# A fused two-block transformer kernel: each feed-forward's down product by seven products for a pair of chunks instead of eight

## The reference, cut to what matters

```python
# first block: x is 272 x 1024 (16 meta tokens ahead of 256), D_FF = 2816
h = rms_norm(x, ffn_norm_g[l])
g = jnp.einsum('bld,df->blf', h, w_gate[l])
u = jnp.einsum('bld,df->blf', h, w_up[l])
x = x + jnp.einsum('blf,fd->bld', jax.nn.silu(g) * u, w_down[l])
return x[:, N_META:]
# second block: D_FF_2 = 4096
n2 = rms_norm_2(h, norm_mlp_pre[l])
hid = jnp.square(jax.nn.relu(jnp.einsum('bsd,df->bsf', n2, w_up[l])))
mlp_out = jnp.einsum('bsf,fd->bsd', hid, w_down[l])
h = h + rms_norm_2(mlp_out, norm_mlp_post[l])
```

## Time and profile before

| | us |
|---|---|
| time, median of 3 runs (lowest to highest) | 759.55 (758.77 to 761.12) |
| the profiled execution's own time | 758.59 |
| its span, first to last instruction | 757.3 |
| PE busy | 739.8 (98%) |
| DVE, ACT, POOL busy | 457.8, 373.3, 112.5 |
| first feed-forward's products, start to end | 131.0 to 321.0 |
| second feed-forward's products, start to end | 570.2 to 751.5 |

### The profile page before, as it was taken

How to read it: one execution, slowest core, us unless ns; L and a number is a source line. 1 busy time by engine, 2 the same in 40 slices (tenths; PEclk the granted TensorE clock), 3 DMA queues, 4 the chain that set the end, 5 groups by cost and what they waited for, 6 DMA issues and landing times.

```text
span 757.3 us, 11043 instructions
## 1 busy us (share of the span) xinstructions
PE 739.8 (98%) x4394; PEld 641.1 (85%) x4394; DVE 457.8 (60%) x635; ACT 373.3 (49%) x535; POOL 112.5 (15%) x138
## 2 busy tenths in 40 slices
PE   6999999999999999999999999999999999999996
PEld 5877778999999999888888888888779899998895
DVE  5898695766555555465747555674948754455433
ACT  6666754644444434285443534664338644444431
POOL 2867550100000000001110000000302111001110
PEclk9999999999999999999999999999999999999999
DMA  9642142787665666446536543474535766656511
GB/s 318 207 132 82 58 160 92 229 284 220 189 212 172 195 216 208 133 142 219 169 110 195 194 139 112 123 250 147 178 107 198 260 192 187 206 184 191 180 46 56
DMA packets 70179, 130.46 MB, mean 172 GB/s; under 512 B 5312, under 2 KB 29072, under 8 KB 70128
## 3 DMA queue, kind: packets, MB, share of 16 engines
q1 hardware_dynamic: 68144, 125.00, 52.3%
q0 software_dynamic: 1552, 4.20, 1.7%
q10 hardware_dynamic: 432, 0.56, 0.2%
HBM read 128.62 MB, written 1.05 MB: 171 GB/s over the span
## 4 chain that ended last, share of the span: by engine, by line
PE 93%; DVE 3%; DMA 2%; issue 1%; ACT 1%; SPq 0%; DVEq 0%; ACTq 0%
PE psum L453 41%; PE psum L888 29%; PE psum L506 12%; PE psum L930 2%; DMA w_raw<-in_w_in 2%; PE psum L680 1%; PE psum L601 1%; PE psum L546 1%; PE psum L631 1%; PE psum L1058 1%; PE psum L582 1%; PE psum L652 1%; DVE b_ratio L2154 0%; PE psum L992 0%; PE psum L1020 0%
## 5 line engine op out<-in xcount | busy, mean ns | idle before, releaser
L1908 DVE TENSOR_TENSOR w_lo<-w_raw,w_hi 128x1024 fp32r<-128x1024 f32 x225 | 275.2, 1235 | 158.3 <-ACT w_hi L1284 157.7
L1284 ACT ACTIVATE w_hi<-w_raw 128x1024 fp32r<-128x1024 f32 x231 | 241.2, 1059 | 180.7 <-PE psum L888 78.6
L888 PE MATMUL psum<-h_hi,w_hi 128*128 128x256 f32 x608 | 170.3, 284 | 0.6 <-issue 0.6
L888 PE MATMUL psum<-h_hi,w_lo 128*128 128x256 f32 x608 | 169.5, 283 | 0.0
L888 PE MATMUL psum<-h_lo,w_hi 128*128 128x256 f32 x608 | 161.8, 281 | 0.0
L888 PEld LDWEIGHTS psum<-h_hi,w_hi 128*128 128x128 f32 x608 | 114.7, 189 | 1.7 <-issue 0.7
L888 PEld LDWEIGHTS psum<-h_hi,w_lo 128*128 128x128 f32 x608 | 114.4, 188 | 0.0
L888 PEld LDWEIGHTS psum<-h_lo,w_hi 128*128 128x128 f32 x608 | 111.1, 189 | 0.7
L453 PE MATMUL psum<-w_hi,h_hi 128*128 128x512 f32 (+1 forms) x240 | 94.5, 394 | 0.0
L453 PE MATMUL psum<-w_hi,h_lo 128*128 128x512 f32 (+1 forms) x240 | 93.0, 387 | 0.0
L453 PE MATMUL psum<-w_lo,h_hi 128*128 128x512 f32 (+1 forms) x240 | 92.9, 387 | 0.0
(11 more groups left out here) (303 smaller groups left out, 992.7 us busy)
## 6 DMA issues: line engine op xcount, KB each, us to landing
w_raw<-in_w_in SPq DMA_DIRECT2D x77, 512.0 KB, 4.5
w_raw<-in_w_down SPq DMA_DIRECT2D x54, 512.0 KB, 4.3
w_raw<-in_w_up SPq DMA_DIRECT2D x32, 512.0 KB, 4.4
w_raw<-in_w_gate SPq DMA_DIRECT2D x44, 256.0 KB, 2.9
w_raw<-in_w_up SPq DMA_DIRECT2D x44, 256.0 KB, 3.4
w_raw<-in_w_out SPq DMA_DIRECT2D x16, 512.0 KB, 4.0
w_raw<-in_w_branch_a SPq DMA_DIRECT2D x4, 512.0 KB, 4.6
w_raw<-in_w_branch_b SPq DMA_DIRECT2D x4, 512.0 KB, 4.6
```

The costliest lines, as they stand in the source:

```text
L888: mm = pe.matmul(outs, x[:, cols], y[:, kc, :], start=kc == 0 and n == 0, stop=kc == KC - 1 and n == (1 if i == 0 else 2))
L1284: act.activation(T.w_hi[:, k % SLOTS, :], T.w_raw[:, k % RAW_SLOTS, :], ACT.Copy).then_inc(S.w_rounded, 1)
L1908: dve.tensor_tensor(T.w_lo[:, k % SLOTS, :], T.w_raw[:, k % RAW_SLOTS, :], T.w_hi[:, k % SLOTS, :], ALU.subtract).then_inc(S.w_cut, 1)
```

## The change

Two chunks of the inner width (a pair), two halves of the tokens and two halves of the output make a 2 x 2 by 2 x 2 block product. Before, it takes eight products of 128 x 128 by 128 x 512; now it takes seven, in the manner of Strassen and Winograd, of sums and differences of the blocks. The last pair of each feed-forward still takes eight (`down_quarters`).

- **Weights.** `w_down` is laid out as four quarters of 128 x 512 a pair (`quarters`). POOL loads them: three as they are (`load_pair`, 768 KB), the fourth twice (`load_twice`, 512 KB written), and on these two it adds the first two by a transfer that accumulates (`add_pair`, `accum_op`, 512 KB). DVE makes two more sums (`sum_pair`, `sum_pair_rest`). So ACT rounds and DVE cuts seven matrices of 512 columns in three parts (`round_pair`, `cut_pair`: 1536, 1024 and 1024 columns), where it had been two fills of 1024. The results lie in two buffers of their own; the fills now have 4 slots in a feed-forward.
- **Hidden rows.** DVE makes four differences (`sum_hidden`, `_2`, `_3`), ACT rounds and DVE cuts seven blocks (896 columns).
- **PSUM.** Products use banks 0 to 6, and the up products, laid out in fills of one 128-column group, have bank 7 alone. ACT copies it out (`take_up`, in the second block relu by `take_hidden`; the square is now ACT's too), and PE waits for that (`up_taken`) before the next pair of groups.
- **The start of a feed-forward** (`up_first`) works through two banks first: it needs the first and second fill at once and then, after a quarter of the work, the third and the fourth.
- **The ends.** Four of the last products are closed (`MIXED`), and DVE makes the output quarters from the seven sums (`form`, `add_x`) while PE does the three others and the last pair. In the first block three quarters are done before PE turns `x`, and the fourth after.

The diff, cut to its core (without the blank lines):

```diff
+        for f in range(2 * PAIRS1):
+            self.first["up1", f] = len(self.fills)
+            for w in range(2):
+                self.fills.append([(lambda raw: raw, a["up1"][f, :, w, :])])
...
+PRODUCT = {1: (1, 0, 2), 2: (3, 2, 0), 3: (7, 1, 1), 4: (2, 6, 6), 5: (5, 3, 5), 6: (6, 5, 3), 7: (4, 4, 4)}
+EARLY, LATE, MIXED, OWN = (1, 2, 3), (7, 5, 6, 4), (1, 6, 7, 5), (4, 2, 3)
+NEEDS = {1: 1, 2: 1, 3: 1, 7: 2, 5: 2, 6: 3, 4: 3}
+QUARTERS = {1: ((0, 0, 6), (1, 0, 0), (1, 1, 1), (0, 1, 7)), 2: ((0, 0, 6), (0, 1, 7), (1, 0, 0), (1, 1, 1))}
+def pair_place(q):
+    i = q if q <= LAST1 else q - FIRST2
+    return (i + 1) % 2, i % 2
...
-        def multiply_down(i, first):
-            for c in range(chunks):
-                k = W.first[down, i] + c
-                pe.wait_ge(*W.cut(S, k))
-                if c % 2 == 0:
-                    pe.wait_ge(S.hidden_cut, cut0 + i * cut_per + c // 2 + 1)
-                mm = chunk(T.hid_hi[i % 2], T.hid_lo[i % 2], k, 0, 1, c, ((4, 5), (6, 7)), WIDE, first and c == 0, False)
-                mm.then_inc(S.w_used, 1)
...
-            if i > 1:
-                pe.wait_ge(*taken(i - 1))
...
+    def up_first(name, ready, rounded, spread, right=None):
+        k0 = W.first[name, 0]
+        for s, two in ((0, 0), (1, 0), (0, 1), (1, 1), (2, 0), (2, 1), (3, 0), (3, 1)):
+            ks = (k0 + 2 * two, k0 + 2 * two + 1)
+            if s == 0:
+                for k in ks:
+                    pe.wait_ge(*W.cut(S, k))
...
+    def down(q, products, first=False, last=False):
+        buf, i = pair_place(q)
+        pe.wait_ge(S.hidden_cut, q + 1)
+        for n_product, p in enumerate(products):
+            x, y, b = PRODUCT[p]
+            pe.wait_ge(S.pair_cut, pair_parts(q) + NEEDS[p])
+            x_hi, x_lo = T.hid_hi[:, i, x - 1, :], T.hid_lo[:, i, x - 1, :]
+            y_hi, y_lo = T.pair_hi[buf][:, y, :], T.pair_lo[buf][:, y, :]
+            for n, (u, v) in enumerate(((x_hi, y_hi), (x_hi, y_lo), (x_lo, y_hi))):
+                mm = pe.matmul(bank[b][:], u, v, start=first and n == 0, stop=last and n == 2)
+            if last:
+                mm.then_inc(S.product_done, 1)
+        if products == LATE:
+            mm.then_inc(S.pair_used, 1)
+    def down_quarters(block, some):
+        q = (LAST1, LAST2)[block - 1]
+        buf, i = pair_place(q)
+        pe.wait_ge(S.hidden_cut, q + 1)
+        pe.wait_ge(S.pair_cut, pair_parts(q) + 2)
+        for t, half, b in some:
+            if b == 7:
...
+    up_first("up1", CUT["h2"], NORM["h2"], True, turn_x_right)
+    up_two(W.first["up1", 2], 3)
+    pe.wait_ge(S.up_taken, 2)
+    up_two(W.first["up1", 3], 7)
+    up_two(W.first["up1", 4], 6)
+    for i in range(2, PAIRS1):
+        if i == 2:
+            pe.wait_ge(S.spread_copied, 1)
+        else:
+            pe.wait_ge(S.up_taken, 2 * i)
+            up_two(W.first["up1", 2 * i], 7)
+        down(i - 2, EARLY, first=i == 2)
+        pe.wait_ge(S.up_taken, 4 if i == 2 else 2 * i + 1)
+        up_two(W.first["up1", 2 * i + 1], 7)
+        if i == 2:
+            pe.wait_ge(S.up_taken, 5)
+        down(i - 2, LATE, first=i == 2)
+    down(LAST1 - 1, MIXED, last=True)
+    down(LAST1 - 1, OWN)
+    down_quarters(1, QUARTERS[1][:3])
+    turn_pairs(T.x, (0, 1), (5, 6), [[(S.x_added, 9)], [(S.x_added, 10)]])
+    down_quarters(1, QUARTERS[1][3:])
...
+    up_first("up2", CUT["h4"], NORM["h4"], False)
+    up_two(W.first["up2", 4], 3)
+    for i in range(2, PAIRS2):
+        if i > 2:
+            pe.wait_ge(S.up_taken, 2 * PAIRS1 + i)
+            up_two(W.first["up2", 2 * i], 7)
+        else:
+            pe.wait_ge(S.up_taken, 2 * PAIRS1 + 2)
+        down(FIRST2 + i - 2, EARLY, first=i == 2)
+        if i == 2:
+            pe.wait_ge(S.up_taken, 2 * PAIRS1 + 3)
+        down(FIRST2 + i - 2, LATE, first=i == 2)
+    down(LAST2 - 1, MIXED, last=True)
+    down(LAST2 - 1, OWN)
+    down_quarters(2, QUARTERS[2])
...
+    def round_pair(q, part):
+        buf, i = pair_place(q)
+        if part == 0:
+            act.wait_ge(S.pair_landed[i], pair_loads(q))
+            if q == 1:
+                act.wait_ge(S.w_used, W.first["up1", 2])
+            elif q == FIRST2:
+                act.wait_ge(S.quarter_done, 4)
+            elif q == FIRST2 + 1:
+                act.wait_ge(S.w_used, W.first["up2", 4])
+            elif q > 1:
+                act.wait_ge(S.pair_used, pairs_used(q - 1))
+        elif part == 1:
+            act.wait_ge(S.pair_added[i], pair_adds(q))
+        else:
+            act.wait_ge(S.pair_summed, pairs_summed(q) + 1)
...
+    def take_up(j):
+        act.wait_ge(S.w_used, W.first["up1", j] + 2)
+        if j > 1:
+            act.wait_ge(S.hidden_done, j - 1)
+        src = T.psum[:, 4 + 2 * j:6 + 2 * j, 0:SEQ] if j < 2 else halves({2: 3, 4: 6}.get(j, 7))
+        act.activation(T.rows[:, j % 2, :].rearrange("p (c n) -> p c n", c=2), src, ACT.Copy).then_inc(S.up_taken, 1)
...
+    for i in range(1, PAIRS1):
+        round_pair(i - 1, 0)
+        take_up(2 * i)
+        round_fill(f + 4 * i + 4)
+        silu(2 * i)
+        round_fill(f + 4 * i + 5)
+        round_hidden(i - 1)
+        round_pair(i - 1, 1)
+        round_pair(i - 1, 2)
+        if i == LAST1:
+            round_quarters(LAST1, 0)
+            round_quarters(LAST1, 1)
+        take_up(2 * i + 1)
+        round_fill(f + 4 * i + 6)
+        silu(2 * i + 1)
+        round_fill(f + 4 * i + 7)
...
+    def sum_pair(q):
+        i = pair_place(q)[1]
+        dve.wait_ge(S.pair_cut, pair_parts(q) + 1)
+        dve.wait_ge(S.pair_added[i], pair_adds(q))
+        step(dve.tensor_tensor(T.pair_raw[i][:, 0, :], T.pair_t[:, i, 0, :], T.pair_raw[i][:, 1, :], ALU.add))
+    def sum_pair_rest(q):
+        i = pair_place(q)[1]
+        own()
+        dve.tensor_tensor(T.pair_raw[i][:, 2, :], T.pair_raw[i][:, 0, :], T.pair_raw[i][:, 2, :],
+                          ALU.add).then_inc(S.pair_summed, 1)
+    def sum_hidden(q, done):
+        h = T.hbuf[:, pair_place(q)[1]]
+        dve.wait_ge(S.hidden_done, done)
+        if q > 1:
+            dve.wait_ge(S.hidden_cut, q - 1)
+        step(dve.tensor_tensor(h[:, 4:6, :], h[:, 0:1, :].broadcast_to([P, 2, P]), h[:, 1:3, :], ALU.subtract))
...
+    for i in range(1, PAIRS1):
+        sum_hidden(i - 1, 2 * i)
+        cut_pair(i - 1, 0)
+        sum_hidden_2(i - 1)
+        scale_gate(2 * i)
+        sum_hidden_3(i - 1)
+        cut_fill(f + 4 * i + 4)
+        sum_pair(i - 1)
+        times_up(2 * i)
+        sum_pair_rest(i - 1)
+        cut_fill(f + 4 * i + 5)
+        cut_hidden(i - 1)
+        cut_pair(i - 1, 1)
+        cut_pair(i - 1, 2)
+        if i == LAST1:
+            cut_quarters(LAST1, 0)
+            cut_quarters(LAST1, 1)
+        scale_gate(2 * i + 1)
+        cut_fill(f + 4 * i + 6)
+        times_up(2 * i + 1)
+        cut_fill(f + 4 * i + 7)
+    cut_hidden(LAST1)
...
+    p1, u, v21, v22, v12 = T.form[1]
+    dve.wait_ge(S.first_copied, 1)
+    form(1, 2, 3, p1, u, ALU.subtract)
+    step(add_x(p1, 1, 0))
+    own()
+    form_minus(1, 3, 4, u, v21)
+    form(1, 4, 5, u, v12)
+    own()
+    step(add_x(v21, 0, 0))
+    form(1, 4, 5, v21, v22, ALU.subtract)
+    step(add_x(v12, 1, 1))
+    own()
+    step(add_x(v22, 0, 1))
+    for n, (t, half, b) in enumerate(QUARTERS[1]):
+        dve.wait_ge(S.quarter_done, n + 1)
+        own()
+        add_x(bank[b][:], t, half).then_inc(S.x_added, 1)
...
+    round_fill(f + 4)
+    round_pair(FIRST2, 0)
+    round_fill(f + 5)
+    round_pair(FIRST2, 1)
+    round_pair(FIRST2, 2)
+    take_hidden(0)
+    take_hidden(1)
+    square_hidden(0)
+    square_hidden(1)
+    round_fill(f + 6)
...
+            round_pair(q, 0)
+            round_hidden(q)
+            round_pair(q, 1)
+            if k < len(W.fills):
+                round_fill(k)
+            round_pair(q, 2)
+            take_hidden(i)
+            square_hidden(i)
+            if k < len(W.fills):
+                round_fill(k + 1)
...
+    def end_last(n):
+        t, half, b = QUARTERS[2][n]
+        dve.wait_ge(S.quarter_done, 4 + n + 1)
+        own()
+        dve.tensor_tensor(T.last[t, half], bank[b][:], T.last[t, half], ALU.add).then_inc(S.formed, 1)
...
+    end_last(0)
+    scale_last(0)
+    end_last(1)
+    scale_last(1)
+    post_mean(1, 0)
+    end_last(2)
+    post_add(1, 0, HALVES)
+    scale_last(2)
+    end_last(3)
+    scale_last(3)
+    post_mean(1, 1)
+    post_add(1, 1, HALVES)
...
-    for n, (dst, src) in enumerate(two):
-        pool.wait_ge(S.w_used, W.first["up1", 1 + n])
-        pool.dma_start(dst, src, allow_slow_non_contiguous=True).then_inc(S.consts_landed, 16)
+    def load_const(n):
+        dst, src = two[n]
+        pool.wait_ge(S.w_used, W.first["up1", 2 + 2 * n])
+        pool.dma_start(dst, src, allow_slow_non_contiguous=True).then_inc(S.consts_landed, 16)
+    def load_twice(q):
+        i, n = pair_place(q)[1], 1 if q in (LAST1, LAST2) else 2
+        if q == 0:
```

(36 more changed lines are left out.)

526 lines of the change are left out of this document (312 added, 214 removed).

## The result

The changed kernel takes 796.57 us (median of 4 runs, 793.99 to 799.65) beside 760.34 for the kernel before on the same chip: a ratio of 1.0485, 95% interval 1.0434 to 1.0537. One of the four executions of the kernel before took 2571.8 us, and the ratio leaves it out; the other three have a median of 759.55. I had said 769, within 752 to 790. The direction was right, the size was not: the profiled execution is 38.6 us longer (795.9 against 757.3), where my sum had 10.2.

What follows compares the result with a forecast made beforehand. PE, busy 98% of the span, was taken to bound the kernel. 757.3 + 9.6 (first block) + 0.6 (second block) = 767.5 us of span, 768.8 with 1.3 around it, 769 for the median; range 752 to 790.

Steps and rivals of the forecast that it cites:

- The removed work: Both feed-forwards: 75 fewer down matmuls on PE at 0.2325 us, 17.4 us saved (7.0 and 10.5 by block).
- the first block's loop: First feed-forward: sum, cuts, loads, adding transfer, next sum; 17.0 us a turn, 0.6 over PE's step.
- transfer part: In the first block's loop: 3.2 MB at 390 GB/s, 8.2 us of the turn.
- 1.4 us more: First block's loop: upper bound if the addition moves its bytes twice, giving 18.3 us a turn.
- my 9.6: First block's net loss: 4.3 + 4.2 + 4.4 + 3.7 - 7.0 = +9.6 us.
- The rival that I had priced at 788: Accumulating transfers dear or engines saturated: first block's loop at 18.9 us, +19 on the forecast; chance 0.18.
- The addition for this pair is not later: Second feed-forward's first pair: POOL free at about 580, addition lands near 592, no loss booked.
- the tail: End of the second block: store done 9.9 us after PE's last matmul, +4.1 us (2.8 if forms are early).
- Fill 3: Start of the second feed-forward: PE wants it at 573.1, DVE has cut it at about 575.6; +2.5 us.
- The third group's copy: Second feed-forward's start: first pair's four late products wait for ACT's third take, +4.5 us.
- The first, additions in time: Rival: first block's loop under 16.4 us, about 756; chance 0.28, its far end (745) 0.07.
- The third, DVE as the bound: Rival: second block's DVE, 9.6 of 10.65 us a pair, exceeds 100%; 773; chance 0.47 together with the forecast.

Runs made afterwards that it cites:

- run 11: Changed kernel with first-block additions behind own loads, second feed-forward's first two pairs loaded earlier, ACT/DVE copies, last hidden rows and fill 3 reordered: 751.57 us, ratio 0.9899.
- run 2: Changed kernel with the adding transfer made a plain one of the same bytes, the addition itself left out: 777.66 us, ratio 1.0241.
- run 8: As run 1, but with plain transfers of the same bytes for the adding ones, the addition left out: 766.03 us, ratio 1.0093.
- run 4: Changed kernel with the second feed-forward's first pair loaded and added ahead of the last constant and two cuts: 788.33 us, ratio 1.0386.
- run 1: Changed kernel with each first feed-forward addition issued behind its own pair's loads, not the next pair's: 766.01 us, ratio 1.0093.

## Why the prediction was wrong

**The removed work was right** (75 x 0.2325 us). In the second feed-forward a pair takes 10.57 us against my 10.65:

```profile
644.56 4.89 PE psum L1010 x21
649.45 5.69 PE psum L964 x48
655.14 4.78 PE psum L1010 x21
```

With most of the waits gone (run 11), the 17.4 us of PE work removed leave 7.4 us by the medians (758.99 - 751.57).

**The step that failed: the length of the first block's loop.** The mechanism was named with its links, and its serial part fits: from the landing to the addition's issue I had 7.25 us, the trace has 165.18 - 157.78 = 7.4 from DVE's first sum on. The term that was mis-sized is the transfer part, "8.2" and 17.0 in all. Issue to landing was 9.65 us by my sum and 9.9 to 13.7 in the trace, mean 11.2 over ten. What stood behind it is, for the most part, accumulation: I had bounded it from above by "1.4 us more" a turn and taken nothing of that; it measured 1.35 a turn (run 2), 1.28 us of engine time an addition. My bound was right and my choice in it was not, made on a plain transfer's landing, which says nothing on accumulating. With plain transfers the turn is 17.44 us (run 2), so of the 1.8 us by which it was longer than my 17.0 only 0.4 are left for all else: 0.15 for the serial part, and the rest for the rate. I had let 3.2 MB pass at 390 GB/s, the best two microseconds of a trace with short bursts. In the changed kernel, where the engines are nearly full, it is 267 GB/s at a share of 0.90, or 297 at a share of 1:

```profile
640.00:720.00 80.00, 80.00 (x531) 73.38 (x530) 72.37 (x83) 56.31 (x63) 16.24 (x23) 1.00 0.90 267
```

The Trainium skill (DMA: Bandwidth & Descriptors, Where 436 GB/s comes from) has some 358 GB/s as what HBM gives one core; the two best windows of the earlier trace rows are above that, and the fastest stretch of 40 us that I read, in run 11, has 305 at a share of 0.99. The 297 hold the dear additions already: without them the same 80 us have 269 GB/s at a share of 0.78, or 345 at a share of 1 (run 8). So the low rate is in the main the price of accumulating seen once more, and the two are not to be added. With 297 GB/s the 3.2 MB take 10.8 us instead of 8.2, and the loop would have come out at 19.5 us, over the trace; with 390 it came out under it.

In numbers: the tenth addition was to land at 156 + 9 x 17.0 = 309 and landed at 326.8, 1.7 us from the first landing (157.7) and 16.1 from nine turns of 18.8. From there to the turn of x I had 21.6 us and the trace has 18.3, so the end was 3.3 us cheaper than I said: 1.7 + 16.1 - 3.3 = 14.5, the difference between 24.1 and my 9.6. The rival that I had priced at 788, dear accumulation with a loop of 18.9 us, is the one that came for this block; I gave it 0.18.

**The step that was missing: the middle of the second block.** "The addition for this pair is not later" is true; I looked for what the pair's loads would be late for and not for what they would delay. I had read POOL's root at 577 us and never placed the loads ahead of it beside SP's w_out fills, though they issue at the same time: a term that my sum puts at nothing. From z's start to the turn of x it was 256.0 us against 246.2, 9.8 us more. Together with 1.0 between the first block's turn of x and z's start that is 10.8 of the second block's 14.5; run 4 gives back 8.2 of the 9.8.

**The start of the second feed-forward and the tail were right.** Fill 3: 2.5 us said, 2.4 measured. The third group's copy: 4.5 said, 4.9 measured. The end: the last matmul ends at 786.6 of 795.9, 9.3 us behind it where I said 9.9. With -10.5 for the matmuls that is +0.3 against my +0.6. The remaining 3.4 us of the block fit the clock, which I had not in the sum at all. In the kernel before it is granted in full to the end. Behind the new waits it falls, and work that isn't waiting for anything is then longer. Behind the wait for fill 3 stand 72 up matmuls in 10.32 us, 1.7 more than at 0.120 us; the first late products are 12 matmuls in 5.21 us, 2.4 more than at 0.2325 us; together 4.1, enough for the 3.4:

```profile
610.00:620.00 10.00, 9.27 (x65) 9.30 (x66) 9.07 (x11) 4.99 (x6) 2.88 (x3) 0.83 0.77 238
```

```profile
610.73 10.32 PE psum L964 x72
...
633.67 5.21 PE psum L1010 x12
```

So each of these three waits (6.2, 2.4 and 4.9 us) cost more than itself: behind each there is such a stretch.

**The other rivals.** The first, additions in time, is what run 1 made of the kernel: I said 756 for it, and it was 766, of which 8 are the collision in the middle. The third, DVE as the bound, is seen only at one place: in run 11 from 588 to 607 us the chain is almost all DVE, which goes round in 9.6 and 9.5 us a pair, as my 9.6 has it, and PE waits 2.4 us in all for ACT's copies behind it.

## What to carry to other kernels

When a transfer's issue depends on work that depends on the transfer before, lay out the circle and add it up with the rate of a long busy stretch and the dearest bound of an operation that no trace shows: an error of 10% in one turn is paid in each. Moving one issue in a queue can be worth more than the arithmetic saved; here the place of the addition was worth 30 us and the removed matmuls 17. For every load that a change adds, look for what lies in the same microseconds on other queues, not only for who waits for it.

## What the runs showed of the hardware

An accumulating transfer of 0.52 MB held the DMA engines for 1.26 to 1.28 us longer than a plain one (some 1.8 times as long, runs 2 and 8). At a busy share of 0.9 for 80 us the engines moved 267 GB/s with these transfers among them, not the 384 to 400 of the earlier trace rows; without accumulation 269 at a share of 0.78 (run 8). A 512 KB fill that lands in 5.0 us in run 4 took 12.4 (medians of four) beside 1.8 MB that POOL had issued within 2 us. PE's granted clock, full in all slices of the page before, was 0.64 to 0.85 in the ten-microsecond windows in or behind which PE had waited for 2.4 to 6.2 us.
